# The handover from the first feed-forward to the sparse attention, by token tile: both key chunks first, as rows of tokens that are turned afterwards

## The reference

```python
# end of layer 0
h = h + rms_norm_2(swiglu_ffn(normed, ffn_w_in[0], ffn_w_out[0]), ffn_norm_post[0])
# start of layer 1
kv = rms_norm_2(h, kv_norm) @ kv_w
k_c, v_c, k_s, v_s, k_w, v_w = [t.reshape(B, S, G, d) for t in jnp.split(kv, 6, axis=-1)]
normed = rms_norm_2(h, mix_norm_pre[1])
proj = normed @ w_in          # q of 16 heads, and three gates a head
```

## Time and profile before

| | us |
|---|---|
| median of three runs | 1220.99 (1220.68 to 1221.53) |
| the profiled execution, its own time | 1221.12 |
| its span | 1219.10 |
| TensorE matmul busy | 1185.5 |
| VectorE busy | 758.5 |
| ScalarE busy | 600.0 |
| GpSimd busy | 151.6 |
| mean granted TensorE clock | 0.992 |

### The profile page before, as it was taken

The page is one execution under the profiler, slowest core; times in us unless marked ns, Lnnn a source line. Parts: engine busy times, 40 slices in busy tenths (PEclk is TensorE's granted clock), DMA queues, the critical chain, the costliest instruction groups (busy, mean ns, idle before and its releaser), DMA issues.

```text
span 1219.1 us, 19296 instructions
## 1 busy us (share of the span) xinstructions
PE 1185.5 (97%) x7504; PEld 1052.2 (86%) x7504; DVE 758.5 (62%) x1049; ACT 600.0 (49%) x862; POOL 151.6 (12%) x175
## 2 busy tenths in 40 slices
PE   6999999998999999999999999999799989999997
PEld 6999999997888887888888888888799968888885
DVE  5667544376887555564535777764676866777752
ACT  6665553434544444543434544443566756445431
POOL 2000000051123001211100111100101101111100
PEclk9999999999999999999999999999899999999999
DMA  9455344543555654645435455465444234554540
GB/s 355 176 208 190 105 139 173 176 168 139 178 202 177 245 184 160 227 160 186 173 133 212 156 176 195 180 220 194 146 153 160 70 109 173 211 198 172 179 166 34
DMA packets 31975, 212.06 MB, mean 174 GB/s; under 512 B 4169, under 2 KB 4829, under 8 KB 7592
## 3 DMA queue, kind: packets, MB, share of 16 engines
q1 hardware_dynamic: 28936, 201.68, 46.6%
q0 software_dynamic: 2688, 9.26, 2.2%
q10 hardware_dynamic: 288, 0.23, 0.1%
HBM read 210.08 MB, written 1.08 MB: 173 GB/s over the span
## 4 chain that ended last, share of the span: by engine, by line
PE 86%; issue 6%; DVE 3%; ACT 2%; POOL 2%; DMA 1%; SPq 0%; DVEq 0%; POOLq 0%; ACTq 0%
PE acc L446 41%; PE acc L585 17%; PE acc L587 8%; PE aux L446 8%; PE acc L486 1%; POOL gate L795 1%; PE acc L488 1%; PE acc L490 1%; PE acc L539 1%; PE acc L536 1%; PE acc L541 1%; PE aux L2579 1%; PE aux L2640 1%; PE aux L2228 1%; ACT wh L419 1%
## 5 line engine op out<-in xcount | busy, mean ns | idle before, releaser
L427 DVE TENSOR_TENSOR wl<-raw,wh 128x2048 fp32r<-128x2048 f32 x129 | 295.2, 2294 | 259.7 <-ACT wh L419 253.0
L419 ACT ACTIVATE wh<-raw 128x2048 fp32r<-128x2048 f32 x190 | 362.7, 1912 | 144.9 <-PE acc L446 109.9
L585 PE MATMUL acc<-hx,wh 128*128 128x512 f32 x864 | 305.4, 399 | 0.0
L587 PE MATMUL acc<-hx,wl 128*128 128x256 f32 x864 | 242.7, 281 | 0.0
L446 PE MATMUL acc<-hx,wh 128*128 128x256 f32 x1280 | 234.6, 285 | 1.9 <-DVE hx L662 1.9
L446 PEld LDWEIGHTS acc<-hx,wh 128*128 128x128 f32 x1280 | 200.7, 193 | 3.4 <-DVE wl L427 2.1
L585 PEld LDWEIGHTS acc<-hx,wh 128*128 128x128 f32 x864 | 162.4, 188 | 40.4
L446 PE MATMUL acc<-hx,wl 128*128 128x256 f32 x640 | 181.7, 284 | 0.0
L587 PEld LDWEIGHTS acc<-hx,wl 128*128 128x128 f32 x864 | 163.2, 189 | 0.0
L434 DVE TENSOR_TENSOR wl<-raw,wh 128x1024 fp32r<-128x1024 f32 x122 | 151.9, 1245 | 1.5 <-ACT wh L419 1.0
L446 PEld LDWEIGHTS acc<-hx,wl 128*128 128x128 f32 x640 | 123.3, 193 | 0.0
(11 more groups left out here) (382 smaller groups left out, 1948.2 us busy)
## 6 DMA issues: line engine op xcount, KB each, us to landing
raw<-in_stream SPq DMA_DIRECT2D x190, 1024.0 KB, 4.8
bias_b<-in_bias POOLq DMA_DIRECT2D x6, 512.0 KB, 4.6
grow<-in_grows POOLq DMA_DIRECT2D x4, 512.0 KB, 4.3
nbias<-strip POOLq DMA_DIRECT2D x4, 512.0 KB, 4.6
x<-in_x SPq DMA_DIRECT2D x2, 512.0 KB, 4.0
y<-x SPq DMA_DIRECT2D x1, 1024.0 KB, 3.9
s<-cums POOLq DMA_DIRECT2D x1, 512.0 KB, 4.2
decay<-in_decay POOLq DMA_DIRECT2D x1, 512.0 KB, 3.8
```

The costliest lines, as they stand in the source:

```text
L419: nc.scalar.activation(wh[:, s, :], raw[:, s, :], ACT.Copy).then_inc(hi_ready, 1)
L427: nc.vector.tensor_tensor(wl[:, s, :], raw[:, s, :], wh[:, s, :].bitcast(F32), ALU.subtract).then_inc(lo_ready, 1)
L585: nc.tensor.matmul(out[:, :], wh[:, s, cols], hx[:, k].rearrange("p a n -> p (a n)"), start=(k == 0), stop=False, skip_group_check=True)
L587: last = nc.tensor.matmul(out[:, 0:SEQ], wl[:, s, cols], hh[:, k, :], start=False, stop=(k == KT - 1), skip_group_check=True)
```

## The change

- `ffn_out_0`: chunks 6 to 8 of the second half run for both tiles, the last two for tile 0 and then for tile 1. `ffn_out_1` keeps its order.
- `post(1)` and the norm for both tiles are replaced by the helpers by token tile, on all engines. `mixed2`, `grow2` and `fjunk` move to another place in SBUF.
- The attention's chunks begin with `ks`, `kw`, `q0`, `q1`. `ks` and `kw` are the two early chunks by token tile (`early_n` with `kvh`, `kvl`). Their results have tokens on partitions: ScalarE copies them to `kn` (`kn_take`), TensorE turns them into `aux[5]` and `aux[4]` with eight transposes (`turn_keys`, between the halves of `q0`), VectorE copies them to `ksw` (`k_take`).
- The query part `hh`, `hl` of the norm follows after the key part of tile 1, for both tiles together, with eight operations of 128x256 on each of the two engines.
- The loads of `w_gate` and `pe_in` are issued by ScalarE after `tile_post`, where they were issued after the last square of `ffn_out_0`.
- In the batches, the product halves `vs`, `vs`, `vw`, `vw` take the places of `kw`, `kw`, `vs`, `vs`, `vw`, `vw`, and the lists of splits on ScalarE and VectorE are reordered.

```diff
-NSA_CHUNKS = ("ks", "q0", "q1", "kw", "vs", "vw", "q2", "kc", "q3", "vc", "ck0", "ck1", "cv0", "cv1")
+NSA_CHUNKS = ("ks", "kw", "q0", "q1", "vs", "vw", "q2", "kc", "q3", "vc", "ck0", "ck1", "cv0", "cv1")
...
-                for i in range(5):
-                    product_w(pe, o0 + 6 + i, g0 + 2, hid2h, hid2l, 2 + WKT * i, WKT, FFN_KT, second=True)
+                def second_half(i, toks=(0, 1)):
+                    product_w(pe, o0 + 6 + i, g0 + 2, hid2h, hid2l, 2 + WKT * i, WKT, FFN_KT, toks=toks, second=True)
+
+                for i in range(3):
+                    second_half(i)
+                for toks in ((0, 1),) if layer else ((0,), (1,)):
+                    for i in (3, 4):
+                        second_half(i, toks)
...
-            norm_pe(pe, 1)
+            c, g = NSA_CHUNK["ks"], NSA_GROUP["ks"]
+            tile_pe(pe, 3, 3, 0)
+            early_n(pe, c, g, kvh, kvl, 3, 0, ((1, 1, 4), lambda: tile_pe(pe, 3, 3, 1)))
+            early_n(pe, c, g, kvh, kvl, 3, 1)
+
+            def turn_keys():
+
+                for i in range(2):
+                    nsa_out_of(pe, ("ks", "kw")[i])
+                    for s in range(2):
+                        for t in range(TT):
+                            c0 = s * SEQ + t * P
+                            tr = nc.tensor.transpose(aux[:, 5 - i, c0:c0 + P], kn[:, i, t, s * P:(s + 1) * P], ident[:])
+                    tr.then_inc(kn_turned, 1)
...
-                nsa_out_of(pe, ("ks", "kw")[kind])
+                pe.wait_ge(keys_out, kind + 1)
...
-            nsa_t("ks", kvh, kvl, normed(12))
-            nsa_t("q0", hh, hl, normed(12 + KT))
+            nsa_t("q0", hh, hl, normed(12), (0,))
+            turn_keys()
+            nsa_q("q0", 1)
             pe.wait_ge(wg_ready, 2)
+            pe.wait_ge(keys_out, 2)
...
-            nsa_k("kw", 0)
+            nsa_v("vs", 0)
             scores_of("s1")
-            nsa_k("kw", 1)
+            nsa_v("vs", 1)
             probs_turn("s0")
 
-            nsa_v("vs", 0)
+            nsa_v("vw", 0)
             scores_of("w0")
-            nsa_v("vs", 1)
-
-            nsa_v("vw", 0)
             values_of("s0")
             nsa_v("vw", 1)
             probs_turn("s1")
```

ScalarE and VectorE:

```diff
-            post(1, "ffn_out_0", (6, 5), fjunk, 1)
...
+            tile_post(1, 1, "ffn_out_0", 6, fjunk, START["nsa"] + 2, kvh)
             for dst, src in ((w_gate[:], io["w_gate"]), (pe_in[:], io["pe_in"])):
                 act.dma_start(dst, src).then_inc(nsa_const, 16)
-            norm_act_squares(act, 1, lambda t: [(post_done, TT + t + 1)])
...
+            for k in range(KT):
+                if k % 2 == 0:
+                    act.wait_ge(tile_lo, 16 * 3 + KT + k + 2)
+                a.activation(hh[:, k, :], aux[:, k // 2, (k % 2) * SEQ:(k % 2 + 1) * SEQ], ACT.Copy,
+                             scale=gains[:, 4, k:k + 1]).then_inc(norm_hi, 1)
...
-            stage_hi(3, 4)
+            kn_take(0)
+            kn_take(1)
+            stage_hi(3)
             q_take(0)
-            stage_hi(5)
+            stage_hi(4)
...
-            stage_hi(6)
+            stage_hi(5, 6)
             exps_of("s1")
...
+            tile_post(1, 1, "ffn_out_0", 6, mixed2, grow2, START["nsa"] + 2, kvl, kvh)
+            lo_part(4, hl, hh, 12)
...
+            k_take(0)
+            k_take(1)
             stage_lo(3)
-            kv_take("ks", ksw[:, 0])
-            stage_lo(4, 5)
             scores_take("s0")
+            stage_lo(4)
...
             probs_take("s0")
+            stage_lo(5)
+            scores_take("s1")
+            kv_take("vs", vsw[:, 0])
+            probs_take("s1")
             stage_lo(6)
-            scores_take("s1")
-            kv_take("kw", ksw[:, 1])
-            probs_take("s1")
+            scores_take("w0")
             stage_lo(7)
-            scores_take("w0")
-            kv_take("vs", vsw[:, 0])
             probs_take("w0")
             stage_lo(8)
             kv_take("vw", vsw[:, 1])
```

More of the change, by code:

```diff
@@ L535, in part @@
                     if lo:
-                        last = nc.tensor.matmul(out, hl[:, k, tok], wh[:, s, cols], start=False, stop=(k == KT - 1),
+                        last = nc.tensor.matmul(out, al[:, k, tok], wh[:, s, cols], start=False, stop=(k == KT - 1),
                                                 skip_group_check=True)
                         continue
-                    nc.tensor.matmul(out, hh[:, k, tok], wh[:, s, cols], start=(k == 0 and t == 0), stop=False,
+                    nc.tensor.matmul(out, ah[:, k, tok], wh[:, s, cols], start=(k == 0 and t == 0), stop=False,
                                      skip_group_check=True)
-                    nc.tensor.matmul(out, hh[:, k, tok], wl[:, s, cols], start=False, stop=False, skip_group_check=True)
+                    nc.tensor.matmul(out, ah[:, k, tok], wl[:, s, cols], start=False, stop=False, skip_group_check=True)
                 if t and lo:
@@ L877, in _ @@
             ffn_pool(0)
-            post(1)
-            norm_pool(pool, 1)
+            tile_post(1)
             pool.wait_ge(mm_done, START["nsa"])
@@ L923, in _ @@
             load(growb[:], io["grows"][3:4, :].broadcast_to([P, D]), grow_in[3])
-            tile_post(1)
+            tile_post(2)
             pool.wait_ge(post_done, 3 * TT)
@@ L1220, in tile_x_square, with tile_post @@
                                  accum_out=sums[:, 2 * t + half:2 * t + half + 1]).then_inc(x_sq, 1)
-            def tile_post(m, n, name, slot, junk, ahead):
+            def tile_post(m, n, name, slot, junk, ahead, dst=hh):
                 tile_square(n, name, 1, 0, junk)
@@ L1277, in _, with kn_take @@
             ffn_act(0)
-            post(1, "ffn_out_0", (6, 5), fjunk, 1)
-            act.wait_ge(mm_done, START["nsa"])
+            o0 = START["ffn_out_0"]
+            for c in range(o0 + 4, o0 + 9):
+                split_hi(act, c)
+            for t in range(TT):
+                tile_square(1, "ffn_out_0", 0, t, fjunk)
+            for c in range(o0 + 9, o0 + 13):
+                split_hi(act, c)
+            tile_post(1, 1, "ffn_out_0", 6, fjunk, START["nsa"] + 2, kvh)
             for dst, src in ((w_gate[:], io["w_gate"]), (pe_in[:], io["pe_in"])):
                 act.dma_start(dst, src).then_inc(nsa_const, 16)
-            norm_act_squares(act, 1, lambda t: [(post_done, TT + t + 1)])
[L1284 to L1291, removed]
+            for k in range(KT):
[3 more added lines that the diff above has]
+                             scale=gains[:, 4, k:k + 1]).then_inc(norm_hi, 1)
+            def kn_take(i):
+                g = NSA_GROUP[("ks", "kw")[i]]
+                act.wait_ge(mm_done, NSA_CHUNK[("ks", "kw")[i]] + 1)
+                a.activation(kn[:, i].rearrange("p t n -> p (t n)"), acc[g % 2][:], ACT.Copy).then_inc(acc_out[g % 2], 1)
             def stage_hi(*chunks):
@@ L1428, in _ @@
             stage_hi(19)
[L1429 removed]
+            tile_post(2, 2, "nsa_out", 5, nsq, START["ffn_in_1"] + LATE)
             ffn_act(1)
@@ L1902, in tile_xn, with tile_post @@
                 v.tensor_scalar(xn[:, t, :], x[:, t, :], stat[:, t, 7:8], None, ALU.mult).then_inc(xn_out, 1)
-            def tile_post(m, n, name, slot, mixed, grow, ahead):
+            def tile_post(m, n, name, slot, mixed, grow, ahead, dst=hl, hi=hh):
                 tile_mix(n, name, 1, 0, mixed, grow)
@@ L1961, in _ @@
             ffn_dve(0)
[L1962 to L1965, removed]
+            o0 = START["ffn_out_0"]
+            dve.wait_ge(grow_in[2], 16)
+            for c in range(o0 + 4, o0 + 9):
+                split_lo(dve, c)
+            for t in range(TT):
+                tile_mix(1, "ffn_out_0", 0, t, mixed2, grow2)
+            for c in range(o0 + 9, o0 + 13):
+                split_lo(dve, c)
+            tile_post(1, 1, "ffn_out_0", 6, mixed2, grow2, START["nsa"] + 2, kvl, kvh)
+            lo_part(4, hl, hh, 12)
             def windows_take(i):
@@ L1996, in kv_take, with k_take @@
                 v.tensor_copy(dst.rearrange("p t n -> p (t n)"), acc[g % 2][:]).then_inc(acc_out[g % 2], 1)
+            def k_take(i):
+                dve.wait_ge(kn_turned, i + 1)
+                v.tensor_copy(ksw[:, i].rearrange("p s n -> p (s n)"), aux[:, 5 - i, :]).then_inc(keys_out, 1)
             def raw_take(j):
```

37 lines of the change are left out of this document (21 added, 16 removed).

## The result

The changed kernel takes **1213.01 us** (median of 4 runs, 1212.01 to 1213.77) against 1221.11 for the kernel before (4 runs, 1220.68 to 1221.53). The ratio is 0.9938, with a 95% interval of 0.9925 to 0.995: 8.1 us faster by the medians. The profiled execution took 1212.43, its span is 1210.3. The forecast was 1214.2 with a range of 1212.8 to 1216.6.

The account below looks back on a forecast made before the run. TensorE, busy 97% of the span, was taken as the bound. Handover gain 7.35, less 0.05 wait before `q0` and 0.4 attention lag, gave 6.9: from 1221.12 to 1214.2 us, range 1212.8 to 1216.6.

Parts of the forecast that it names:

- The handover: From `ffn_out_0` to the attention: token tile 0's norm runs beside tile 1's matmuls; 27.95 us becomes 20.60, gain 7.35.
- The turning: Eight transposes of the keys, all on TensorE's path, cost 0.87 us.
- What stands before `q0`: ScalarE's `hh` casts and copy of `ks` to `kn` delay `q0` by 0 to 0.2 us; 0.05 charged.
- rival C: Before `q0`: ScalarE's casts, DMA issues and `kn` copy come 1 us late, giving 1215.2; chance 0.10.
- rule on small tiles: Skill's rule that many small tiles each pay a fixed part, so by-token halves eat margins; 4.36 for 3.08.
- The wait for the keys: Key copies on VectorE end at 884.0, before TensorE ends `q0` at 885.4: margin 1.4 us, no wait.
- The attention's lag: VectorE comes 0.5 us late to `w1`, little is recovered, 0.4 shows at `V s3`; bounds 0 to 2.
- Rival B: In the attention VectorE falls 2 to 3 us behind, costing another 1.5 to 2.4: 1215.7 to 1216.6; chance 0.14.
- A: The forecast itself, whole kernel: 1214.2 us, own range 1213.3 to 1215.2; chance 0.71.
- D: At the handover the token split frees nothing early, it stays 10.0 and turned keys add 0.9: 1222; chance 0.02.
- E: In the by-token stretch TensorE is granted only 1.2 GHz, 13.5 us more: 1227.7; chance 0.03, milder form included.

Follow-up runs that it names:

- e1: Changed kernel, but `ffn_out_0`'s last two chunks go over both token tiles at once again; 1217.04 us (8 runs).
- e3: Kernel before, with 45 matmuls of 256 columns, adding no result, in the handover's idle time; 1219.57 us (11 runs).
- e2: Changed kernel without the turning of the keys: eight transposes, two VectorE copies and their wait left out; 1212.44 us (5 runs).
- e7: Changed kernel with the keys turned behind both halves of `q0` instead of between them; 1215.07 us (4 runs).
- e4: Kernel before with only the attention's new order of chunks and lists, old handover kept; 1220.23 us (10 runs).
- a0_again: Changed kernel run again, unaltered, for a second profile; 1212.11 us (5 runs).
- b0_again: Kernel before run again, unaltered, for a second profile; 1220.93 us (10 runs).
- a1_again: Changed kernel run a third time, unaltered, for one more profile; 1212.45 us (1211.68 to 1213.18).
- e6: Changed kernel with 32 useless matmuls of 256 columns in the four idle times of the attention's tail; 1212.87 us (6 runs).

## Why the prediction was right, and where its steps were off

**The handover: right, for its reasons.** The early stretch was forecast as 13.85 by laying the one before `ffn_in_0` over it; it took 13.83. Idle before the first transposes 0.3 to 0.4: 0.33. Gain up to there 7.35: 7.38 at `V s3`. It adds up piece by piece. In the kernel before the gates' matmuls, behind `ks` and `q0`, start here:

```profile
886.73 0.40 PE L446 MATMUL aux<-hx,wgh 128*48 128x256 f32 x2
```

886.73 - 864.82 = 21.91 (forecast 10.00 + 12.07 = 22.07); in the changed kernel it is 885.50 - 865.04 = 20.46 (forecast 20.60). Both forecasts are 0.15 long, which cancels; with `kw`, 5.88, the difference is 7.33. Taking apart what the forecast took as one window, e1 and e3 show that no single part carries it: keys by token 4.04, last chunks 2.71, clock 0.63.

**The turning, 0.87: right** (0.85 by e2).

**What stands before `q0`: right.** The `hh` casts ended at 874.20 + 3.08 = 877.28 (forecast 877.25), the copy of `ks` ran from 877.05 to 877.77, and `q0` began with no wait. 0.05 was charged, 0 was paid; rival C (1 us late) falls. The casts whose 4.36 for 3.08 I set beside that rival's rule on small tiles read `aux`, which is PSUM, and the section named there is about operations that read SBUF; so no row here tests that rule, and the two times stand by the earlier trace rows alone.

**The wait for the keys: right**, a margin of 1.8 instead of 1.4, and e7 shows the price once the cover is gone.

**The attention's lag: the step that failed.** I had VectorE coming 0.5 late to `w1`, with little recovered, and 0.4 of it at `V s3`. VectorE's timeline of the changed kernel, `w1` and the next batch:

```profile
921.16 0.28 DVE L2063 CUSTOM_DVE_ANT_0 ns<-aux,nbias 128x128 f32<-128x128 f32 x1
...
928.86 2.29 DVE L431 TENSOR_TENSOR wl<-raw,wh 128x2048 fp32r<-128x2048 f32 x1 [1.25 <-ACT wh L423]
931.14 0.29 DVE L2063 CUSTOM_DVE_ANT_0 ns<-aux,nbias 128x128 f32<-128x128 f32 x1
```

`S w1` ended at 920.88, so it came 0.28 late, and had an idle of 1.25 already in that batch, in front of the next split. My count up to `w1` was off by 0.2 (0.28 for 0.5). From the end of `S s1` (898.91 + 1.58 = 900.49) TensorE took 20.39 to the end of `S w1`, where I had 20.3, and VectorE 20.67 to its start at `w1`, where I had 20.8. The lag was a small difference of two sums of 20 us: had I used for TensorE the 3.07 and 1.31 that the earlier trace rows print, and not my 2.97 and 1.23, TensorE's sum would have been 20.8 and the lag 0. The sentence that little is recovered, since the ring of VectorE and ScalarE takes nearly TensorE's 10.1 for a batch, was wrong: the lag was made up in one batch, with `s2`'s scores taken up at 931.14 when `S s2` ended at 931.08. The term is 0 (e4 and the equal 59.95), which was its lower bound. Rival B falls with it.

**The sum.** 7.38 from the profiled 1221.12 is 1213.74; the forecast had 1214.2. The profiled pair differs by 8.69: 7.38, and 1.67 of low clock in the attention's tail of before, less the 0.22 by which the changed kernel's `ffn_out_0` ended later, less 0.14 at the ends. I took the time before as if its profile held no such fall of the clock. The medians on the three occasions differ by 8.1, 8.8 and 8.1, against 7.38 to 7.72 by the ledger; their intervals (0.9917 to 0.995 in all, 6.1 to 10.1 us) hold both, and what makes the rest isn't shown. Dips can be a part of it: sorted by a run's mean granted clock, 50 runs of the kernel before took on average 1221.1 at 0.992 and 0.993 (16 runs), 1220.6 at 0.994 (27) and 1219.4 at 0.995 and 0.996 (7). But the changed kernel took 1212.3 at 0.996 (9) and 1213.0 at 0.997 (5), so there the runs with more low clock were not the longer ones. Another part can lie in the kernel's start: ScalarE's thirteenth split, about 80 us in, starts between 77.94 (e4) and 81.30 (a0_again) in the thirteen profiles, 3.4 apart, in instructions that the change doesn't touch.

**Where luck comes in.** The handover was forecast by its mechanism. That the first median lies in the range is partly luck. 1213.01 is below my own range for A (1213.3 to 1215.2), in the 0.5 that I had added below it for fewer switches and no lag. The lag was indeed absent, but that is worth 0.4, not the 1.2 between 1214.2 and 1213.01. The medians of the two repetitions, 1212.11 and 1212.45, lie below 1212.8, outside the range. With its 6.9 the forecast was short of all three medians' gains by 1.2 to 1.9, and only 0.5 of that comes from its own terms (0.4, 0.05 and 0.03).

Rivals D (an idle time of 5 us left before the transposes) and E (a clock of 0.5 in the stretch) are excluded by the idle time of 0.33 and the clock of 1.00.

## What to carry to other kernels

A handover in which a norm stands between two products is best costed by laying a window of the same shape from elsewhere in the same trace over it; this one came out within 0.02. Before a pair of times is compared below 1%, compare distances between the same instructions in several profiles: they repeat to 0.03 where the runs spread by 2 to 4, and they show which microseconds are the change's, which are the clock's, and which come from the start. They don't account for all of a difference of medians: in e1 and e7 1 to 2 us were left over. And a transfer or norm that is last in the kernel is worth splitting by tile too: here 2.5 from the last matmul to the end of the span.

## What the runs showed of the hardware that was not expected

The granted clock falls to 1.2 GHz in places where TensorE's idle times are short, in some executions and not in others, with the same instructions. Around 284 to 292, far from any edit, it is 0.79 in four of the thirteen profiles (b0_again, e1, e2, e4) and 1.00 in the others, and costs about 1.6: e2's splits on ScalarE run 0.02 behind those of the changed kernel's first profile at 288 and 1.60 behind at 331. TensorE's idle times just ahead of it are 1.4 and 1.9, in the profiles with the fall as in those without. The stretch in b0_again, then in a1_again:

```profile
284.00:292.00 8.00, 6.10 (x20) 4.58 (x19) 5.39 (x5) 3.14 (x5) 0.00 (x0) 0.79 0.70 262
```

```profile
284.00:292.00 8.00, 6.08 (x28) 4.81 (x27) 5.00 (x5) 3.14 (x5) 0.00 (x0) 1.00 0.70 262
```

In the tail of the attention it is five of thirteen, costing 1.06 to 1.67, with idle times of 0.4 to 2.0 ahead of it; in e6's profile it doesn't fall. In the old handover it fell in all three profiles (before, b0_again, e4), with TensorE standing still; where 45 matmuls filled the time, it did not. Around 12 to 20 it is 0.79 in six of thirteen, all of them without the fall at 284 to 292. This one has no price that shows: the thirteenth split starts at 79.2 to 80.2 in the six with it, and at 77.9 to 81.3 in the seven without. What picks the execution in which it falls is open.
